# Six expert weight pieces read ahead into idle buffers, and copied into the ring by GpSimd

## What is computed

```python
logits = hf @ router_w + router_b
top_val, top_idx = lax.top_k(logits, TOP_K)          # 4 of 32 experts for each token
top_w = jax.nn.softmax(top_val, axis=-1)
...
g = xb @ w_gate[e] + b_gate[e]                       # [tokens of e, 1024] @ [1024, 1024]
u = xb @ w_up[e] + b_up[e]
g = jnp.minimum(g, SWIGLU_LIMIT); u = jnp.clip(u, -SWIGLU_LIMIT, SWIGLU_LIMIT)
act = g * jax.nn.sigmoid(SWIGLU_ALPHA * g) * (u + 1.0)
y = act @ w_down[e] + b_down[e]
```

## Time and profile before

| | |
|---|---|
| median of 3 runs | 2389.74 us (2388.43 to 2390.51) |
| profiled execution, its own time | 2387.88 us |
| its span, first to last instruction | 2385.9 us |
| mean granted TensorE clock | 0.989 |
| PE busy (matmuls) | 2283.3 us, 96% |
| DVE busy | 1053.2 us, 44% |
| ACT busy | 709.7 us, 30% |
| POOL busy | 5.0 us, 6 instructions |
| SP's weight queue | 648.19 MB, 69.0% of 16 DMA engines' span |

### The profile page before, as it was taken

The page is one execution under the profiler, slowest core; times in us unless marked ns, Lnnn a source line. Parts: engine busy times, 40 slices in busy tenths (PEclk is TensorE's granted clock), DMA queues, the critical chain, the costliest instruction groups (busy, mean ns, idle before and its releaser), DMA issues.

```text
span 2385.9 us, 34503 instructions
## 1 busy us (share of the span) xinstructions
PE 2283.3 (96%) x13627; PEld 1553.7 (65%) x13628; DVE 1053.2 (44%) x1458; ACT 709.7 (30%) x959; POOL 5.0 (0%) x6
## 2 busy tenths in 40 slices
PE   6999899999999999999998999989999999999999
PEld 4667833333333333333336999989989899999998
DVE  7666531111111111111116765566565655576654
ACT  2123410110100000011005344364353643445443
POOL 0000000000000000000000000000000000000000
PEclk9999999999999999999999999989999999999999
DMA  9366579979999999899997555545545255544552
GB/s 372 119 223 227 201 321 422 422 327 422 422 422 422 422 422 418 336 422 422 422 422 280 193 187 192 180 171 184 193 169 192 89 187 192 185 177 169 185 193 89
DMA packets 93890, 657.06 MB, mean 275 GB/s; under 512 B 10308, under 2 KB 13144, under 8 KB 14840
## 3 DMA queue, kind: packets, MB, share of 16 engines
q1 hardware_dynamic: 91104, 648.19, 69.0%
q10 hardware_dynamic: 2712, 7.82, 1.0%
HBM read 654.84 MB, written 1.13 MB: 275 GB/s over the span
## 4 chain that ended last, share of the span: by engine, by line
PE 75%; DMA 18%; DVE 3%; ACT 2%; issue 1%; SPq 0%; ACTq 0%; DVEq 0%
DMA ring<-in_w_exp 16%; PE psum L534 13%; PE psum L533 13%; PE psum L535 13%; PE psum L886 13%; PE psum L913 5%; PE psum L703 2%; PE psum L602 2%; PE psum L863 1%; DMA ring<-in_w_mix 1%; PE psum L923 1%; DVE arena L1833 1%; DVE arena L1827 1%; PE psum L1037 1%; PE psum L881 1%
## 5 line engine op out<-in xcount | busy, mean ns | idle before, releaser
L436 DVE TENSOR_TENSOR ring_parts<-ring,ring_parts 128x2048 fp32r<-128x2048 f32 x181 | 414.1, 2291 | 287.9 <-ACT ring_parts L1573 281.1
L534 PE MATMUL psum<-arena_parts,ring_parts 128*128 128x256 f32 x1920 | 540.6, 282 | 0.0
L886 PE MATMUL psum<-ring,arena 128*64 128x512 f32 x2176 | 489.5, 597 | 37.6 <-DMA ring<-in_w_exp 37.5
L533 PE MATMUL psum<-x_parts,ring_parts 128*128 128x256 f32 x1808 | 507.2, 281 | 0.0
L535 PE MATMUL psum<-x_parts,ring_parts 128*128 128x256 f32 x1808 | 506.2, 280 | 0.0
L886 PEld LDWEIGHTS psum<-ring,arena 128*64 128x64 f32 x2176 | 157.4, 137 | 327.7 <-issue 327.7
L1573 ACT ACTIVATE ring_parts<-ring 128x2048 fp32r<-128x2048 f32 x181 | 342.0, 1905 | 87.8 <-DMA ring<-in_w_mix 57.9
L534 PEld LDWEIGHTS psum<-arena_parts,ring_parts 128*128 128x128 f32 x1920 | 360.5, 188 | 1.7
L533 PEld LDWEIGHTS psum<-x_parts,ring_parts 128*128 128x128 f32 x1808 | 340.3, 188 | 1.6
L535 PEld LDWEIGHTS psum<-x_parts,ring_parts 128*128 128x128 f32 x1808 | 341.2, 189 | 0.0
L1830 DVE TENSOR_SCALAR arena<-psum 128x512 f32<-128x512 f32 x68 | 47.0, 691 | 609.8 <-ACT arena L1539 409.6
(11 more groups left out here) (289 smaller groups left out, 2099.5 us busy)
## 6 DMA issues: line engine op xcount, KB each, us to landing
ring<-in_w_exp SPq DMA_DIRECT2D x384, 1024.0 KB, 20.8
ring<-in_w_ffn SPq DMA_DIRECT2D x132, 1024.0 KB, 4.8
ring<-in_w_mix SPq DMA_DIRECT2D x49, 1024.0 KB, 4.8
ring<-in_w_ada SPq DMA_DIRECT2D x24, 1024.0 KB, 6.4
ring<-in_w_in SPq DMA_DIRECT2D x16, 1024.0 KB, 10.6
arena<-gain_scratch ACTq DMA_DIRECT2D x10, 512.0 KB, 4.0
ring<-in_w_out SPq DMA_DIRECT2D x4, 1024.0 KB, 4.8
ring<-in_w_attn SPq DMA_DIRECT2D x2, 1024.0 KB, 4.7
```

What stands on the lines that cost most here:

```text
L436: return engine.tensor_tensor(ring_parts[:, s, :], ring[:, s, :], ring_parts[:, RAW + s, :], ALU.subtract)
L533: mm(out, w[0], a[0], start=start, stop=False, **more)
L534: mm(out, w[0], a[1], start=False, stop=False, **more)
L886: last = mm(psum[side(half), bank, :], hg[:, k, n, :], w[half][:, k * HALF:(k + 1) * HALF], start=False, stop=n == 1 and k == 3, skip_grou ...
```

## The change

1. Six buffers that lie idle during the experts take slot 0's piece (`EXPERT_ORDER[0]`) of experts 26 to 31: a part of `par`, three places of the arena (one buffer is in two halves), the tile `x`, the tile `h`, and a stretch that `pos_i`, `diagonal`, `rstd`, `rstd_x`, `lnv` and `line` share. For the last one these six tiles are laid out side by side; their order in SBUF is all that changes of them.
2. SP fetches them behind expert 0's pieces and ahead of its wait for `tables`: two at once, the third after the third `norm_sums`, the last three after `tokens_turned` is 3 (the second turn of x) and `line_out`.
3. The loop over the experts becomes a loop over 1 to 25 and six expert loads written out, each of slots 1 to 11 alone.
4. POOL waits for the tables and for all seven fetches, then for each of the six experts until the block before has read slot 0, and copies the piece into slot 0. It signals `full[0]` in SP's place.
5. `load_gain(0)`, with its wait, moves from ahead of ACT's expert loop to behind it, as buffer 2 covers its place.

```diff
+SPARE_EXPERTS = (26, 27, 28, 29, 30, 31)
...
+        with nc.sbuf_tensor("front_rows", [P, PIECE], F32) as front_rows:
+            pass
         pos_i = sb("pos_i", [P, T], I32)
+        diagonal = sb("diagonal", [P, 4, P])
+        rstd = sb("rstd", [P, T])
+        rstd_x = sb("rstd_x", [P, T])
+        lnv = sb("lnv", [P, T])
+        line = sb("line", [HEADS2, 2 * T])
...
+        ssm_at = PAR.at["b_re"][0]
+        spare_buffers = ((par[:, ssm_at:ssm_at + PIECE],),
+                         (view(10240, PIECE),),
+                         (view(5120, PIECE // 2), view(3072, PIECE // 2)),
+                         (x[:].rearrange("p k t -> p (k t)"),),
+                         (h[:].rearrange("p k t -> p (k t)"),),
+                         (front_rows[:],))
+        spare_loads = sum(len(buffers) for buffers in spare_buffers)
...
-            sp.wait_ge(sem("tables"), 1)
-            with sp.Fori(1, E) as e:
-                first = sp.value_load(starts[0:1, bass.ds(e, 1)], min_val=1, max_val=BLOCKS)
-                for n in range(EXPERT_PIECES):
+
+            def load_spare(j):
+
+                at_ = 0
+                for part in spare_buffers[j]:
+                    width = part.shape[1]
+                    sp.dma_start(part, io["w_exp"][SPARE_EXPERTS[j] * EXPERT_PIECES + EXPERT_ORDER[0]][:, at_:at_ + width]
+                                 ).then_inc(sem("spare_in"), 16)
+                    at_ += width
+
+            load_spare(0)
+            load_spare(1)
+            sp.wait_ge(sem("norm_sums"), 3)
+            load_spare(2)
+            sp.wait_ge(sem("tokens_turned"), 3)
+            sp.wait_ge(sem("line_out"), 16)
+            load_spare(3)
+            load_spare(4)
+            load_spare(5)
+
+            def load_expert(e, index, slots):
+
+                first = sp.value_load(starts[0:1, index], min_val=1, max_val=BLOCKS)
+                for n in slots:
                     sp.wait_ge(pieces, first * EXPERT_PIECES + (N_PRE + n + 1 - EXPERT_PIECES))
                     sp.dma_start(ring[:, n, :], row("w_exp", e * EXPERT_PIECES + EXPERT_ORDER[n])).then_inc(full[n], 16)
+
+            sp.wait_ge(sem("tables"), 1)
+            for begin, end in zip((0,) + SPARE_EXPERTS, SPARE_EXPERTS + (E,)):
+                if begin:
+                    load_expert(begin, slice(begin, begin + 1), range(1, EXPERT_PIECES))
+                if begin + 1 < end:
+                    with sp.Fori(begin + 1, end) as e:
+                        load_expert(e, bass.ds(e, 1), range(EXPERT_PIECES))
...
-            act.wait_ge(sem("gain_out"), 3 * 16)
-            load_gain(0)
             act.wait_ge(sem("tables"), 2)
...
+            act.wait_ge(sem("gain_out"), 3 * 16)
+            load_gain(0)
             expert_gate(final)
             expert_turned(final)
...
+            pool.wait_ge(sem("tables"), 1)
+            pool.wait_ge(sem("spare_in"), 16 * spare_loads)
+            for j, e in enumerate(SPARE_EXPERTS):
+                first = pool.value_load(starts[0:1, e:e + 1], min_val=1, max_val=BLOCKS)
+                pool.wait_ge(pieces, first * EXPERT_PIECES + (N_PRE + 1 - EXPERT_PIECES))
+                at_ = 0
+                for part in spare_buffers[j]:
+                    width = part.shape[1]
+                    nc.gpsimd.tensor_copy(ring[:, 0, at_:at_ + width], part).then_inc(full[0], 16 * width // PIECE)
+                    at_ += width
```

More of the change, by code:

```diff
@@ L276, in build @@
         cond = sb("cond", [P, KC])
-        diagonal = sb("diagonal", [P, 4, P])
         ada_sum = sb("ada_sum", [P, 4 * P])
         coef = sb("coef", [P, 4, KC])
-        rstd = sb("rstd", [P, T])
-        rstd_x = sb("rstd_x", [P, T])
-        lnv = sb("lnv", [P, T])
         etab = sb("etab", [P, BLOCKS], I32)
@@ L286, in build @@
         nblk = sb("nblk", [P, 2], I32)
-        line = sb("line", [HEADS2, 2 * T])
         lam2 = sb("lam2", [P, 2])
```

## The result

| | before | after |
|---|---|---|
| median of 5 runs | 2389.74 us (2386.35 to 2394.30) | 2372.39 us (2368.85 to 2376.39) |
| profiled execution, its own time | 2387.88 us | 2372.39 us |
| its span | 2385.9 us | 2369.7 us |
| mean granted TensorE clock | 0.989 | 0.992 |

The ratio is 0.9928, 95% interval 0.991 to 0.9946: faster by 17 us, between 12.9 and 21.5. I had forecast 13.7 us, 2376.0, with a range from 2374.0 to 2380.5. One of the 54 timed executions of the kernel before in this study was slow, 3286.88 us, and counts in no ratio and no mean.

The account below looks back on a forecast made before the run. The DMA queue was taken to bound the last stretch of the expert loop; six pieces removed give 14.92 us, less 1.25 for the late gain fetch, so 13.67 us off 2389.74: 2376.0 us, range 2374.0 to 2380.5.

Parts of the forecast that it names:

- What bounds the last stretch: Late blocks of the expert loop: PE waits for the DMA queue and is 14.28 us late at the last block.
- Front fetches at no cost: Six fetches in the queue's standstill before the first reload cost 0, bounds 0 and 3 us.
- The late gain fetch: load_gain(0) in the full queue near the loop's end delays expert 31's last pieces 1.25 us, bounds 0 and 1.6.
- the sum: The smaller of the queue's gain, 14.92 - 1.25 = 13.67 us, and what PE can take, 14.28.
- The copies: POOL's copies into slot 0 during a block: 4.75 us each, 23.3 us free, cost 0.
- The slower rival: Long POOL copies hold up DVE's gate operation in six blocks; at 19 us each, 2432 us in all; chance 0.04.
- The loop as a whole: The expert loop with all terms gains 13.7 us.
- the 0.7 us for the runs' spread: Allowance for differences between runs within the forecast's own interval, 2374.8 to 2377.2 us, chance 0.75.
- the median of the runs is 1.86 us above the profiled one: 2389.74 - 13.7: Final step for the whole kernel: gain subtracted from the median of the runs, giving 2376.0 us.
- behind it the same order stands: Behind the expert loop, the mixer's first piece and y_tok's copy come as much earlier as the loop's end.
- none of the four: Front fetches delay first reload, 0.07; gain fetch or DVE costs more, 0.07; queue not the pacer, 0.07; long copies, 0.04.
- The first half of the second: Late gain fetch costs twice its bytes; with its other half, slight DVE delay, gain 11 to 12.5 us, chance 0.07.

Follow-up runs that it names:

- front_only: The changed kernel without copies: six front fetches waited for but never read, SP fetching all twelve slots, load_gain(0) in its old place; 2386.76 us, ratio 0.9995.
- front_b: The same program as front_only, profiled a second time; first stretch 194.08 us, loop 965.09 us.
- the two refill kernels: The changed kernel with buffers refilled at two queue standstills for later experts, one also with load_gain(0) back ahead of the loop; 2360.43 and 2361.32 us.
- gain_late: The kernel before with one edit, load_gain(0) moved behind the expert loop; 2388.34 us against 2388.26, ratio 1.0002.
- before_b: The kernel before, unchanged, profiled again; loop 967.93 us, 1108.99 us behind the loop.
- the second: Comparison of the changed kernel, unchanged and run once more, with the kernel before; 2374.02 us against 2388.26, ratio 0.9939.
- mid: The changed kernel with the six prefetched pieces used for experts 16 to 21 in place of 26 to 31; 2372.73 us, ratio 0.9946.

## Why the prediction was right and wrong

- **What bounds the last stretch: right.** The queue, with PE late by 14.28 us at its end. Taking six pieces out removed every wait from blocks 29 to 32, three pieces half of it, and six in another stretch the same 14.4 us there.
- **Front fetches at no cost: right within half a microsecond.** The first reload is issued at 312.08, and the first stretch of front_only and front_b is no longer than before. But the queue's dip near 335 us stands in nine of ten profiles with these fetches and in none without, so the term of 0 may be some 0.5 us too low.
- **The late gain fetch: a term that was mis-sized or joined by another loss.** I took 1.25 us from its share of the engines, and the sum left PE a wait of 0.6. The wait was 1.96 us in the first profile of the changed kernel and 1.17 in the second. Pieces behind the fetch landed 1.3 us late by the two refill kernels, as its bytes say, and 2.6 in gain_late, above my upper bound of 1.6. Since before_b and front_only lose 1.4 to 1.6 us at the same pieces without it, whose the surplus is stays open.
- **The copies: right in effect, wrong in size.** 1.89 us, not 4.75. The price by columns of a two-operand subtraction was too high for a copy; nothing depended on it. The slower rival needed copies of 12 us.
- **The loop as a whole: nearly right.** 13.7 forecast. 11.45 in the two first profiles; the means of all profiles (965.93 for three of before, 953.25 for two of the changed kernel) differ by 12.7. PE's longer wait at the last block (0.6 to 1.4 us more than in the sum) is of the size of the missing part.
- **Where it failed: the base that the sum was taken from, and the 0.7 us for the runs' spread.** The step "the median of the runs is 1.86 us above the profiled one: 2389.74 - 13.7" took the median of three executions for the kernel's time, and "behind it the same order stands" let the time behind the loop pass over unchanged, at 0. The 53 executions of the kernel before have a mean of 2387.39 (2380.49 to 2394.30), so the base was 2.35 us too high. Equal programs differ by 4.7 us behind the loop and by 4.6 ahead of it, where I allowed 0.7; of the 16.2 us between the first two profiles, 4.95 came from there. The miss of 3.6 us (2376.0 against 2372.39) is then 2.35 from the base, 0.95 because the five executions of the changed kernel lay below its mean of 2373.35, and 0.3 from the gain itself, 14.0 in the mean against 13.7.
- **The range.** 2374.0 to 2380.5 reached 2 us down and 4.5 up, from rivals that were all on the slow side, and gave the execution itself no part. The first comparison came out at 17.35 us with an interval of 12.9 to 21.5, the second at 14.6 (11.5 to 17.7). Both hold 13.7, so neither contradicts the mechanism; nor does either confirm it to the microsecond. That 14.0 over all executions falls so near 13.7 is partly luck, as the loops differ by 12.7. In hindsight, with spreads of 4.7 and 4.6 us known, a range of some 5 us either way was due, 2371 to 2381. The one profile that I had showed clock dips behind the loop (0.91 in a window), but not that they come and go.
- **Rivals:** none of the four came true as a whole. The first half of the second, a gain fetch at twice its bytes, is what gain_late shows and the refill kernels don't.

What stays open: the queue's losses of 0 to 2 us, in equal programs at the same place, and its dip near 335 us have no cause here. Nor do I know why the loop's 12.7 us and the whole executions' 14.0 (12.3 to 15.8) differ by 1.3; the interval covers it.

## What to carry to other kernels

A queue that feeds a loop at its limit has idle time at the loop's start and wherever the consumer takes two turns on one fill. A fetch moved into such a gap is worth its full transfer time, up to what the consumer waits in the stretch that follows, and it doesn't matter which fetch of that stretch it is. The copy that brings it into place is cheap when it runs on an idle engine and is due a whole block later. When the gain is under one per cent, look in the trace for stretches whose length depends on the granted clock before you set the range: a single profile shows one draw of it, and so does a median of three executions.

## What the runs showed of the hardware that I had not expected

- GpSimd copies 128 x 2048 fp32 values from SBUF to SBUF in 1.89 us, as fast as ScalarE (1.91).
- A fetch of 0.52 MB on another queue, put in among saturated 1 MiB fetches, delayed the landing of the next ones by 1.3 us by the two refill kernels, the time of its bytes, and by 1.2 and then 2.6 us in gain_late, where the surplus can't be told from the queue's own losses (1.4 and 1.6 us in front_only and before_b).
- The time behind the loop went with the lost clock: 1107.85 to 1109.29 us with 4.8 to 8.2 us lost, 1113.05 to 1116.65 with 12.8 to 16.2, and both the kernel before and the changed one stand in both groups.
- A stall of PE of 2.1 to 2.7 us inside a busy stretch was followed in three profiles (front_only, before_b, mid) by matmuls that took 1.6 to 1.7 us more in sum, with a granted clock of 0.83 and 0.60 in the windows of front_only. In gain_late stalls of 2.11 and 2.67 us were not (3.65 us for 16 matmuls behind both).
- DVE instructions with SBUF operands took 0.85 us (one instruction) and 1.3 us (two) longer beside GpSimd copies, and one that read PSUM didn't.
